# Decoder step with a routed channel mixer: each token's row is completed in the expert slot of its second choice, experts are visited across the groups, the weight ring has 20 halves, and both choices are routed in one pass

## The reference, cut to what matters

```python
def finish_layer(...):
    ...
    x = x + mixed @ w_o
    h2 = rmsnorm(x, g_ffn).reshape(-1, D_MODEL)
    return x + hier_moe(h2, ...)
...
    for e in range(N_EXPERTS):                       # hier_moe; gates are 0 but for a token's two experts
        hid = jax.nn.silu(h @ w_gate_e[e]) * (h @ w_up_e[e])
        out = out + gates[:, e:e + 1] * (hid @ w_down_e[e])
...
y_prompt = rmsnorm(xp, g_final)
y_sample = rmsnorm(xs, g_final)
```

## Time and profile before

| | us |
|---|---|
| median of 3 runs | 1323.79 |
| lowest and highest run | 1319.96, 1324.32 |
| span of the profiled execution | 1329.1 |
| VectorE's first instruction of route, TensorE's first expert product | 758.5, 796.5 |
| TensorE's last expert product ends | 1288.5 |
| finish begins to issue | 1299.5 |

### The profile page before, as it was taken

The page is one execution under the profiler, slowest core; times in us unless marked ns, Lnnn a source line. Parts: engine busy times, 40 slices in busy tenths (PEclk is TensorE's granted clock), DMA queues, the critical chain, the costliest instruction groups (busy, mean ns, idle before and its releaser), DMA issues. The chain is left out here.

```text
span 1329.1 us, 13696 instructions
## 1 busy us (share of the span) xinstructions
PE 1131.4 (85%) x5474; PEld 664.0 (50%) x5474; DVE 585.7 (44%) x738; ACT 246.0 (19%) x399; POOL 274.2 (21%) x204
## 2 busy tenths in 40 slices
PE   3999999999987999979999739988888888888770
PEld 3877888888854444436646323333333333333320
DVE  3089999999955646524531351111111111111115
ACT  2022111210223544510021101111111111111112
POOL 1035454554311333310000000111111111111110
PEclk9999999999988999988999859999899998898995
DMA  6969999999837899998937487999999999999935
GB/s 197 383 228 392 363 396 367 406 408 408 315 118 279 330 404 415 398 414 324 285 127 264 166 370 257 413 410 411 412 411 412 413 410 410 409 412 409 412 150 208
DMA packets 104342, 455.71 MB, mean 343 GB/s; under 512 B 13613, under 2 KB 45661, under 8 KB 57445
## 3 DMA queue, kind: packets, MB, share of 16 engines
q1 hardware_dynamic: 72469, 301.43, 58.2%
q0 software_dynamic: 24032, 143.60, 27.6%
q10 hardware_dynamic: 7776, 9.78, 2.2%
HBM read 442.10 MB, written 65.44 MB: 382 GB/s over the span
## 5 line engine op out<-in xcount | busy, mean ns | idle before, releaser
L506 PE MATMUL proj_ps<-hT,w_slots 128*128 128x260 f32 x1472 | 330.2, 384 | 4.9 <-ACT stage L529 2.6
L506 PEld LDWEIGHTS proj_ps<-hT,w_slots 128*128 128x128 f32 x1472 | 278.2, 191 | 55.0 <-issue 11.9
L1852 PE MATMUL ex_gp<-raw,ex_xT 128*64 128x512 f32 x672 | 167.9, 648 | 43.5 <-DMA raw<-in_w_up_e 42.7
L206 POOL DMA_INDIRECT ring<-in_cache_k_a,run_sb x64 | 137.7, 2152 | 196.3 <-DVE scores L574 167.9
L1804 DVE TENSOR_TENSOR ex_hm<-ex_sg,ex_gp 64x512 f32<-64x512 f32 x32 | 21.7, 679 | 342.4 <-ACT ex_sg L1783 342.4
L567 DVE TENSOR_TENSOR ring<-ring,q_rep 128x2048 f32<-128x2048 f32 x64 | 145.8, 2280 | 43.0 <-ACT q_rep L551 40.6
L574 DVE TENSOR_REDUCE scores<-ring 128x32 f32<-128x2048 f32 x64 | 145.6, 2276 | 0.0
L1852 PEld LDWEIGHTS ex_gp<-raw,ex_xT 128*64 128x64 f32 x672 | 55.5, 148 | 140.8 <-issue 133.6
L1852 PE MATMUL ex_gp<-qk,ex_xT 128*64 128x512 f32 x352 | 93.1, 680 | 25.8 <-DMA qk<-in_w_up_e 24.7
L1754 POOL DMA_INDIRECT pair_rows<-ex_yg,ex_to x32 | 29.6, 924 | 407.2 <-PE ex_xp L1838 397.2
L206 POOL DMA_INDIRECT ring<-in_cache_v_a,run_sb x64 | 71.5, 1117 | 170.1 <-PE at_vp L774 151.9
(11 more groups left out here) (260 smaller groups left out, 1053.1 us busy)
## 6 DMA issues: line engine op xcount, KB each, us to landing
raw<-in_w_down_e SPq DMA_DIRECT2D x53, 1024.0 KB, 29.3
raw<-in_w_gate_e SPq DMA_DIRECT2D x42, 1024.0 KB, 28.8
raw<-in_w_up_e SPq DMA_DIRECT2D x42, 1024.0 KB, 28.5
o_kvs<-in_cache_kv_b SPq DMA_DIRECT2D x39, 1024.0 KB
w_slots<-in_w_in SPq DMA_DIRECT2D x23, 1024.0 KB, 12.4
qk<-in_w_gate_e SPq DMA_DIRECT2D x22, 1024.0 KB, 28.3
qk<-in_w_up_e SPq DMA_DIRECT2D x22, 1024.0 KB, 28.4
qk<-in_w_down_e SPq DMA_DIRECT2D x11, 1024.0 KB, 29.5
```

The lines of the kernel that those rows point to most:

```text
L206: pool.indirect_dma_start(k.ring[:, n % RING, :], None, runs, bass.IndirectOffsetOnAxis(ap=k.run[:, i:i + 1], axis=0), bounds_check=runs.s ...
L506: last = pe.matmul(pp[:, j, half, 0:H], w[:, m % W_PARTS, c, j * P:(j + 1) * P], k.hT[:, c, half * H:(half + 1) * H], start=(c == 0), stop ...
L1852: last = pe.matmul(gp[at:at + SLOT, j], xT[:, c, :], raw_slot(k, slot)[:, c1 * FF:(c1 + 1) * FF], start=(c == 0), stop=(c == KC - 1))
```

## The change

Block `finish` is gone, and with it `pairs` and `h2`.

- **merge** stores, instead of `h2`, rows of x with 1/rms appended (1040 numbers, `x_rows`). SP also copies x into a new HBM array `part`, and it waits for `samples_b` before it issues two more weight halves (into the room of `scores` and `oT`), ahead of the eight shift pieces and of the rows.
- **route** treats both choices in one pass with a leading dimension of 2, and sums the counts on VectorE, so that fewer products are needed. A token's entry is marked (`LATER`) in the lower of its two slots. From it come three columns of `index`: the row to gather from `x_rows`, the row of `part` to store to (first choice visited), the row of `part` to gather from and of `y` to store to (second). POOL clears `xg` and issues the first four gathers at the end of this block. Four instructions for `owner` and `n_more` move into experts.
- **experts** are visited as 0, 8, 16, 24, 1, 9, ... . A token's two experts lie in one group, so at least four visits apart. The rows are scaled by 1/rms on the way through TensorE (a product with a diagonal `dg` instead of a transpose) and by `g_ffn` when VectorE, not ScalarE, copies them out. For a token's second visit POOL gathers its `part` row over its x. VectorE adds gate times result to the row in `xg`. Then the row goes to `part` (first visit), or through square, root, reciprocal and product with `g_final` to `yo` and to `y` (second visit). So there are up to four indirect DMAs for each expert, 64 slots each, in place of two.
- The ring has 20 halves, seven of them early, and no longer a whole number of experts.

```diff
-SETS = 3
-RING_W = 6 * SETS
-RAW_EARLY = 5
+RING_W = 20
+RAW_QK = 5
+RAW_EARLY = 7
...
                 sp.wait_ge(s["ya"], KC)
-                load_expert(k, sp, 0, 0, some=range(2))
+                for n in range(2):
+                    load_half(k, sp, n)
+                sp.dma_start(k.io["part"][0:SEQ, :], k.io["x_prompt"][0]).then_inc(k.rows_out, 16)
+                sp.dma_start(k.io["part"][SEQ:TOK, :], x_rows(k, NB)).then_inc(k.rows_out, 16)
                 sp.wait_ge(s["values"], 1)
-                load_expert(k, sp, 0, 0, some=range(2, RAW_EARLY))
+                for n in range(2, RAW_QK):
+                    load_half(k, sp, n)
+                sp.wait_ge(s["yb_s"], 1)
+                for n in range(RAW_QK, RAW_EARLY):
+                    load_half(k, sp, n)
                 shift(k, sp, shift_pieces()[IN_PROJECT + IN_ATTEND + IN_MERGE:])
                 for b in range(NBLK):
                     r = rows_of(b)
                     sp.wait_ge(s["scaled"], b + 1)
-                    sp.dma_start(k.io["h2"][b * P:b * P + r, :], hn(b)[0:r, :]).then_inc(k.h2_out, 16)
-                sp.wait_ge(k.h2_out, 16 * NBLK)
+                    sp.dma_start(k.io["x_rows"][b * P:b * P + r, :], k.x1[0:r, b, :]).then_inc(k.rows_out, 16)
+                sp.wait_ge(k.rows_out, 16 * (NBLK + 2))
...
+def gather_x(k, pool, p):
+
+    pool.indirect_dma_start(k.xg[:, p % XB, :], None, k.io["x_rows"], bass.IndirectOffsetOnAxis(
+        ap=k.index[:, 0, p:p + 1], axis=0), bounds_check=TOK - 1, oob_is_err=False).then_inc(k.x_in[p % XB], 16)
...
             @block.gpsimd
             def _(pool):
+                pool.memset(k.xg[:], 0.0).then_inc(s["cleared"], 1)
                 for sem in done:
                     pool.sem_clear(sem)
+                pool.wait_ge(s["cleared"], 1)
+                pool.wait_ge(s["indexed"], 1)
+                for p in range(XB):
+                    gather_x(k, pool, p)
...
+                def gather_part(p):
+                    pool.wait_ge(s["turned"], p + 1)
+                    pool.wait_ge(a_out[(p - E_GROUPS) % XB], 16 * ((p - E_GROUPS) // XB + 1))
+                    rows(p % XB, x_of(p % XB), k.index[:, 2, p:p + 1], b_in[p % XB])
...
+                for p in range(EXPERTS):
+                    if p >= E_GROUPS:
+                        gather_part(p)
+                    if p >= 2:
+                        store_out(p - 2)
+                        if XB <= p + 2 < EXPERTS:
+                            pool.wait_ge(a_out[(p - 2) % XB], 16 * ((p - 2) // XB + 1))
+                            gather_x(k, pool, p + 2)
+                    if p >= 1:
+                        store_part(p - 1)
+                store_out(EXPERTS - 2)
+                store_out(EXPERTS - 1)
...
+                def root(p):
+                    act.wait_ge(s["added"], p + 1)
+                    if p:
+                        act.wait_ge(s["out"], p)
+                    act.activation(sq[0:SLOT, :], x_of(p % XB), ACT.Square, accum_out=ms[:]).then_inc(s["squared"], 1)
+                    act.wait_ge(s["squared"], p + 1)
+                    act.activation(rms[:], ms[:], ACT.Sqrt, bias=k.const("eps", SLOT), scale=1.0 / D)\
+                        .then_inc(s["roots"], 1)
...
+                def add(p):
+                    if p >= E_GROUPS:
+                        dve.wait_ge(b_in[p % XB], 16 * ((p - E_GROUPS) // XB + 1))
+                    dve.wait_ge(s["y_high"], p + 1)
+                    gate = k.slot_gate[:, p:p + 1]
+                    lo, hi = x_of(p % XB, 0, 512), x_of(p % XB, 512, D)
+                    dve.scalar_tensor_tensor(lo, yp[0:SLOT, p % 2], gate, lo, ALU.mult, ALU.add)
+                    dve.scalar_tensor_tensor(hi, y2[:], gate, hi, ALU.mult, ALU.add).then_inc(s["added"], 1)
+
+                def out(p):
+                    dve.wait_ge(s["roots"], p + 1)
+                    if p:
+                        dve.wait_ge(y_out, 16 * p)
+                    link(dve.reciprocal(rstd[:], rms[:]))
+                    dve.scalar_tensor_tensor(yo[:], x_of(p % XB), rstd[:], gf[:], ALU.mult, ALU.mult)\
+                        .then_inc(s["out"], 1)
...
+                for p in range(EXPERTS):
+                    last = p == EXPERTS - 1
+                    if not last:
+                        diag(p + 1)
+                    else:
+                        add(p - 1)
+                        out(p - 1)
+                    hidden(p)
+                    if not last:
+                        lay_x(p + 1)
+                    lay_h(p)
+                    if p and not last:
+                        add(p - 1)
+                        out(p - 1)
+                add(EXPERTS - 1)
+                out(EXPERTS - 1)
...
+                def turn(j, sem):
+                    v = x_of(j).rearrange("t (p c) -> t c p", c=KC)
                     for c in range(KC):
-                        last = pe.transpose(xp[:, c, :], v[:, c, :], k.const("ident", SLOT)[:, 0:SLOT])
-                    last.then_inc(s["turned"], 1)
+                        last = pe.matmul(xp[:, c, :], v[:, c, :], dg[:], start=True, stop=True)
+                    last.then_inc(sem, 1)
...
-STEPS = [prepare, project, attend, merge, route, experts, finish]
+STEPS = [prepare, project, attend, merge, route, experts]
```

More of the change, by code:

```diff
@@ L70 @@
 FAR = 1e30
-OPEN = 1
+LATER = 1024.0
 NBLK = NB + 1
@@ new lines, in experts @@
+            "out", "counted")}
+        own = k.sem("ex_dve", ctx)
+        more_in = [k.sem(f"mo_in{n}", ctx) for n in range(6)]
+        mo_x, mo_b, mo_a, mo_y = (k.pool_sem("mo_" + n) for n in ("x", "b", "a", "y"))
+        m = {n: k.sem("mo_" + n, ctx) for n in (
+            "free", "scattered", "indexed", "diag", "turned", "x_laid", "hidden", "silu", "h_made", "h_turned",
+            "h_laid", "down", "y_high", "added", "squared", "roots", "inverse", "out")}
+        go_pe, go_pool = k.sem("mo_go_pe", ctx), k.sem("mo_go_pool", ctx)
@@ L1715, in experts @@
-        none = lambda *_: None
+                with eng.Fori(1, MORE + 1) as i:
+                    body(i)
         with nc.Block() as block:
@@ L1731, in _, with body @@
+                def body(i):
+                    e = sp.value_load(k.owner[0:1, bass.ds(i - 1, 1)], min_val=0, max_val=EXPERTS - 1)
+                    sp.wait_ge(m["free"], i)
+                    for n in range(6):
+                        load_matrix(k, sp, n, n, e, more_in[n])
+                more(sp, body)
             @block.gpsimd
             def _(pool):
-                for j in range(2):
-                    pool.dma_start(opened[:, j:j + 1], k.io["g_final"].unsqueeze(0)[:, 0:1]).then_inc(y_out[j], 16)
@@ L1758, in _, with rows @@
-                pool.wait_ge(s["cleared"], 1)
-                for j in range(2):
-                    pool.wait_ge(from_laid[j], 1)
-                    gather(j)
-                passes(pool, none, down, x_next, none)
-                for j in range(2):
-                    pool.wait_ge(y_out[j], 16 * TRIPS + 16)
-                    pool.wait_ge(x_in[j], 16 * (TRIPS + 1))
+                def rows(j, to, index, sem):
+                    return pool.indirect_dma_start(to, None, k.io["part"], bass.IndirectOffsetOnAxis(
+                        ap=index, axis=0), bounds_check=TOK - 1, oob_is_err=False).then_inc(sem, 16)
@@ L1855, in gate_up, with down @@
                                 if c1 == KC // 2 - 1:
-                                    last.then_inc(used[slot], 1)
-                def down(i, j):
-                    pe.wait_ge(s["h_laid"], i * 2 + (j + 1))
-                    which, fill = place(i, j)
-                    for half, slot in enumerate(down_slots(which)):
-                        pe.wait_ge(raw_in[slot], fill * 16)
+                                    after(last, 2 * half + n)
+                def down(j, slots, ready, after):
+                    for half, slot in enumerate(slots):
+                        ready(4 + half)
                         for c1 in range(FC // 2):
@@ new lines, in _ @@
+                pe.wait_ge(s["diag"], 1)
+                turn(0, s["turned"])
+                for p in range(EXPERTS):
+                    last = p == EXPERTS - 1
+                    if last:
+                        down_of(p - 1)
+                    pe.wait_ge(s["x_laid"], p + 1)
+                    gate_up(p % 2, [slot_of(p, n) for n in range(4)], ready(p), after(p))
+                    if p and not last:
+                        down_of(p - 1)
+                    if not last:
+                        pe.wait_ge(s["diag"], p + 2)
+                        turn((p + 1) % XB, s["turned"])
+                    pe.wait_ge(s["h_made"], p + 1)
+                    mix(s["h_turned"])
```

655 lines of the change are left out of this document (340 added, 315 removed).

## The result

The changed kernel takes 1370.82 us (median of 4 runs, 1370.2 to 1372.83) against 1324.05 before: ratio 1.035, interval 1.032 to 1.038, so 46.8 us slower. The forecast was 1317.9 with a range up to 1332. The profiled execution has a span of 1368.4, 45.2 more than the 1323.2 of the sum.

The account below looks back on a forecast made before the run. Weight transfers were taken to bind experts at 410 GB/s, a chain of single steps the end. Start +2.2, rows +13.6, end -21.7 gave -5.9 us: span 1323.2, 1317.9 for the median, range 1304 to 1332.

Parts of the forecast that it names:

- What fits beside the weights: Experts: added TensorE, VectorE, ScalarE and POOL work fits within 15.6 us an expert; TensorE used 13.2 and gets 0.9 more.
- Start of the weights: Merge, route and first expert: steady weight flow starts net 2.2 us later, between -0.8 and +4.8.
- Rows beside the weights: Experts: some 490 more gathered rows at 0.028 us each cost 13.6 us; bounds 4.7 and 25.2.
- The rival by transfer: POOL's queue in 28 visits: each `part` gather costs 0.90 us, filled or not; 25.2 in all, 1329.5; chance 0.18.
- The end: From last down product to end of span: 17.2 us instead of 40.6; after small losses, 21.7 us less.
- the drain: Rival: POOL's drain grows with the number of transfers; 4.8 more at the end, 2.6 in route; 1325.3; chance 0.06.
- The single `yo`: Rival in experts: `out` waits for the store before; if landing doubles, the 16.9 us loop binds; 1335; chance 0.08.
- A fixed price for each transfer: Rival: each indirect transfer takes about 2.0 us of the DMA engines, 114 for 57 more; about 1426; chance 0.01.
- same: Whole kernel: a difference under 0.3% (4 us), hardly told from none; chance 0.26.
- slower: Whole kernel: the changed kernel takes longer than before; chance 0.21.

Follow-up runs that it names:

- e4: Changed kernel with the turn's columns taken side by side instead of 32 bytes apart (columns then meet the wrong weights): 1335.22 us, ratio 1.0077.
- e3: The late scale: changed kernel, complete, turn as 8 transposes, 1/rms applied where gate and up are read: 1334.05 us, ratio 1.0058 to before.
- e6: Kernel of e3 with the 28 gathers from `part` issued but carrying no rows: 1315.34 us, ratio 0.9922.
- e2: Kernel before with one edit: gathered rows turned by a product with the identity instead of transposes: 1385.48 us, ratio 1.0443.
- e5: Kernel of e3 with POOL draining its queue five times within experts: 1323.34 us, ratio 0.9981.
- e7: Kernel of e3 without the 28 gathers from `part`: 1312.66 us, ratio 0.9900.
- e11: Kernel of e3 without the gathers from `part`, its stores to `part` issued without rows: 1308.77 us, ratio 0.9863.
- e12: Kernel of e3 without the gathers from `part` and without the stores to `part`: 1304.46 us, ratio 0.9847.

## Why the prediction was wrong, point by point

- **What fits beside the weights: the step that failed.** "TensorE used 13.2 and gets 0.9 more" was the term. It got 4.6 more: TensorE's chain is 16.95 (8.6 + 3.5 + 3.9 + 0.9), where it had been 12.23 as long as nothing held it. Three things were wrong in the term. I priced 16 float32 products by the 16 of rows 7 (1.95), whose stationary columns lie side by side; the turn's lie 32 bytes apart, which e4 shows to be the whole difference: 2.9 more than the transposes instead of 0.9. I put the clock at nothing and gave no reason: with this turn the granted clock falls in every expert, and gate and up take 8.6 instead of 6.92. And I compared one expert of TensorE (14.1) with one expert of the weights (15.6), where the lead of the ring must be counted: 32 of TensorE's turns against 172 of 192 halves. With 16.95 the first is 542, with 2.86 a half (343.5 / 20 / 6 in e3) the second 492. At the full clock the dear turn would make 15.2 an expert and 486 in all (an estimate from these rows), about even with the weights; by this estimate it is the clock that tips the balance. No rival had TensorE as the bound, though its busy share was the second number that I read.
- **Start of the weights: right, and in part by luck.** `index` stood 21 us after the start of route (20.6 forecast) and experts began 36.1 after it (36). But the parts compensate. The fourth gather landed 35.6 after the start of route, not 33: it took 10.9 from its issue (785.46 to 796.32), where rows 3 have 7.5. The drain ended 0.2 after that landing (783.05 + 13.47 = 796.52), not 3. The first turn took 4.07 and not 2.0, and merge came at 760.7 instead of 763.

```profile
L1505 POOLq DRAIN  x1: 13469/13469/13469, 783.1 to 783.1; - x1
```

- **Rows beside the weights: the mechanism right, the size near.** The rows and not the bare transfers cost it: 18 us (e3 to e6, 13 to 23) for 13.6. The rival by transfer was refuted with empty transfers.
- **The end: right but for the drain**, which was in the rivals with 0.06: 9.77 for 5.60, so 4.2 more where that rival had 4.8. Its 2.6 in route did not come.
- **The single `yo`** bound nothing in the changed kernel. Once the weights bind again it holds `hidden` of expert 31 back by 3.0 (1294.94 to 1297.97), where 0.8 was taken.
- **A fixed price for each transfer**, the rival beside which the Trainium skill (DMA: Bandwidth & Descriptors, Anatomy of one DMA) was named with about 2.0 us: 28 empty gathers and 31 empty stores cost nothing that can be told beyond their part of the drain, so what such a transfer takes by itself is waiting, and no time of the DMA engines. The sum beside that rival should read 1432 (1317.9 + 114) and not 1426; and the chances of "same" and "slower" add up to 0.25 and 0.22, not 0.26 and 0.21.

With the turn as transposes the sum is nearly there: 1317.9 + 4.2 (drain) + 4.4 (rows) + 2.2 (`hidden`) = 1328.7, against 1.0058 x 1324 = 1332 for the late scale. The difference is just within its interval (1328 to 1335).

## What to carry to other kernels

Before a small step is put on an engine that has slack, add up that engine's whole chain for one turn, waits included, and price the step by a row with the same operand layout, not only the same shape. Then look at the granted clock of what follows the step: here a third of the price stood in the products behind it. Compare the chain with the bound over the whole loop: a bound that has a lead from a filled ring needs to run for less than all turns, so an engine that is only just slower throws the lead away. Where two engines are both full, the list of waits says which binds; and where GpSimd issues many DMAs, look at its drain at the end of the block, and drain where it can wait for the last landing.

## What the runs showed of the hardware

- A float32 product whose stationary columns lie 32 bytes apart: 0.24 us an instruction with 64 moving columns; side by side 0.125 (2.00 / 16). Transposes of the same spaced columns: 8 in 1.1.
- With 16 such spaced instructions in every expert the granted clock of TensorE fell to 1.2 GHz once an expert, although it was busy 16.63 of 16.85 us (e2); with transposes in their place the first eight experts ran at 1.00 (e3).
- POOL's drain, when all its transfers have landed: 0.05 us and 0.082 for each transfer since the last drain, also for those that landed long before (0.29 behind 3, 9.77 behind 119). When one is under way, it lasts until that has landed: 8.3 to 9.4 us in e5.
- Rows of 4 KB gathered into 64 partitions beside a full stream of weights cost three to five times their bytes (18 us for about 490, 13 to 23); rows stored from there cost about their bytes (4.2 us by the traces of e7 and e11, 4.9 by the ratios).
- An indirect DMA of 64 slots without any row took nothing off the weights' rate that could be told (469.2 and 469.1 us from the first silu to the last in e11 and e12).
